# Convolution inputs ahead of the forget gates, rotary products behind them: the order of the input projections

## The reference

```
h = x * (1 + scale1) + shift1
p = h @ w_in[l]                     # 3088 columns: qa 512, ka 128, va 128, qkv_b 768, g_b 256,
                                    # beta/alpha 16, f_fw 256, f_bw 256, i_c 256, q_c 256, g_c 256
qkv_b = silu(short_conv(qkv_b, conv_w))              # width 5, centred, per channel
f = lb + (1 - lb) * sigmoid(z);  log_f = log(f)      # z = (f_fw, f_bw); in layer 0 lb = 0
o_a = attn_latent(rope_2d(qa), rope_2d(ka), va, cache_k, cache_v, sink)
x = LayerNorm(alpha*x + gate1 * (concat(attention, gated DeltaNet, HGRN2) @ w_out[l]))
x = LayerNorm(alpha*x + gate2 * FFN(...))            # layer 0 SwiGLU, layer 1 top-2 of 8 experts
```

## Time and profile before

| | us |
|---|---|
| median of 3 runs | 2377.2 (2377.14 to 2379.05) |
| the profiled execution, its span | 2378.1 |
| input projection of layer 0, from 67 to 235 us | 168 |
| attention of layer 0, with the rest of `w_mod`, from 235 to 365 us | 130 |
| input projection of layer 1, from 1156 to 1317 us | 161 |
| TensorE busy over the span | 2118.8 (89%) |
| VectorE, ScalarE, GpSimd busy over the span | 1449.5, 1283.3, 754.2 |

### The profile page before, as it was taken

The page is one execution under the profiler, slowest core; times in us unless marked ns, Lnnn a source line. Parts: engine busy times, 40 slices in busy tenths (PEclk is TensorE's granted clock), DMA queues, the critical chain, the costliest instruction groups (busy, mean ns, idle before and its releaser), DMA issues.

```text
span 2378.1 us, 54636 instructions
## 1 busy us (share of the span) xinstructions
PE 2118.8 (89%) x23130; PEld 1305.1 (55%) x23130; DVE 1449.5 (61%) x1797; ACT 1283.3 (54%) x1665; POOL 754.2 (32%) x556
## 2 busy tenths in 40 slices
PE   5999787978989999999899878878869999999994
PEld 3756456745565555555675558645544444444442
DVE  3254656668261221215558667595379999999985
ACT  3443554556453333423543665465368877778763
POOL 0332115433404242423233236422023333333332
PEclk8999898988999999999999989998979999999997
DMA  9352680020303131315231000100456777990014
GB/s 285 121 174 77 212 285 28 4 58 8 106 17 106 53 106 53 106 53 166 77 103 39 1 10 4 41 21 22 140 223 223 238 265 276 330 335 34 36 65 183
DMA packets 215529, 278.48 MB, mean 117 GB/s; under 512 B 28321, under 2 KB 188941, under 8 KB 215183
## 3 DMA queue, kind: packets, MB, share of 16 engines
q1 hardware_dynamic: 203776, 243.60, 31.5%
q0 software_dynamic: 8432, 29.89, 3.4%
q10 hardware_dynamic: 3103, 1.85, 0.3%
HBM read 368.36 MB, written 29.11 MB: 167 GB/s over the span
## 4 chain that ended last, share of the span: by engine, by line
PE 53%; issue 16%; DVE 13%; POOL 8%; ACT 7%; DMA 2%; SPq 1%; POOLq 0%; DVEq 0%; ACTq 0%
PE ps L2328 50%; POOL mix L1000 6%; DVE mix L1695 1%; DVE arena L1687 1%; DVE mix L1687 1%; DMA wbuf<-in_w_mod 1%; POOL mix L1003 1%; DVE small L1910 1%; DVE arena L1691 1%; SPq L727 1%; DVE mix L1849 1%; DMA const<-in_w_mod 1%; ACT mix L1461 1%; PE ps L3097 1%; PE ps L3073 1%
## 5 line engine op out<-in xcount | busy, mean ns | idle before, releaser
L2328 PE MATMUL ps<-hT,mix 128*128 128x512 f16 (+2 forms) x3024 | 376.7, 287 | 25.0 <-DVE hT L1687 11.8
L2328 PE MATMUL ps<-w,xgT 128*128 128x512 f16 x1632 | 366.3, 381 | 5.3 <-DVE w L2228 5.3
L2228 DVE SCALAR_TENSOR_TENSOR w<-wst,w 128x2048 f16<-128x2048 f32 x136 | 309.8, 2318 | 25.6 <-ACT w L1558 25.5
L2328 PEld LDWEIGHTS ps<-hT,mix 128*128 128x128 f16 x3024 | 227.1, 99 | 172.9 <-issue 22.2
L1032 POOL TENSOR_TENSOR a<-aval,a 128x256 f16<-128x256 f32 x68 | 158.3, 2328 | 370.4 <-ACT a L1606 370.4
L2328 PEld LDWEIGHTS ps<-w,xgT 128*128 128x128 f16 x1632 | 157.7, 98 | 184.5 <-issue 9.6
L1558 ACT ACTIVATE w<-wst 128x2048 f16<-128x2048 f32 x136 | 251.5, 1898 | 9.6 <-DMA xs_rows<-htok,slot_i 9.6
L2328 PE MATMUL ps<-mix 128*128 128x512 f16 (+5 forms) x1856 | 204.7, 288 | 15.7 <-POOL mix L1003 8.8
L2328 PE MATMUL ps<-hT,arena 128*128 128x128 f16 (+1 forms) x1440 | 200.7, 300 | 1.1 <-DVE const L1687 1.1
L2328 PE MATMUL ps<-w2m,aT 128*128 128x512 f16 x816 | 187.2, 379 | 3.8 <-DVE aT L2266 3.8
L2328 PEld LDWEIGHTS ps<-mix 128*128 128x128 f16 (+3 forms) x1856 | 121.3, 123 | 90.4 <-POOL mix L1003 12.4
(11 more groups left out here) (359 smaller groups left out, 3546.3 us busy)
## 6 DMA issues: line engine op xcount, KB each, us to landing
wst<-in_moe_w SPq DMA_DIRECT2D x204, 1024.0 KB
wbuf<-in_w_mod SPq DMA_DIRECT2D x40, 1024.0 KB
wbuf<-in_ffn_w SPq DMA_DIRECT2D x33, 1024.0 KB
wbuf<-in_w_in SPq DMA_DIRECT2D x20, 1024.0 KB
xs_rows<-in_table SPq DMA_DIRECT2D x17, 512.0 KB, 6.4
ys_rows<-yb POOLq DMA_DIRECT2D x17, 512.0 KB, 4.2
wbuf<-in_w_out SPq DMA_DIRECT2D x32, 256.0 KB
xg<-xs_rows POOLq DMA_DIRECT2D x16, 512.0 KB, 5.5
```

What stands on the lines that cost most here:

```text
L2228: v_.scalar_tensor_tensor(out=q[1], in0=staged(s, p), scalar=WS, in1=q[0], op0=ALU.mult, op1=ALU.subtract).then_inc(sg["m_lo13"], 1)
L2328: return mm_(o, w, x, start=first, stop=last, skip_group_check=True)
```

## The change

```diff
-MOD_AT = {j: i for i, j in enumerate(("va", "f0b", "f1b", "b1", "b3", "b5", "gb1", "ckt"))}
-TURN_AT = {"b3": 0, "gc0": 1}
-MOD_FETCH = {"f0": 0, "f1": 1, "b0": 2, "b1": 3, "b2": 4, "ba": 5, "i": 6, "gc": 7}
+MOD_AT = {j: i for i, j in enumerate(("va", "b1", "b3", "b5", "f0b", "f1b", "gb1", "ckt"))}
+TURN_AT = {"f0b": 0, "gc0": 1}
+MOD_FETCH = {"b0": 0, "b1": 1, "b2": 2, "f0": 3, "f1": 4, "ba": 5, "i": 6, "gc": 7}
...
-        j = [f"q{t}" for t in range(4)] + ["ka", "va", "f0a", "f0b", "f1a", "f1b"] + [f"b{t}" for t in range(6)]
-        j += ["gb0", "gb1", "ba", "ia", "ib", "kout", "ckt"] + [f"rot{t}" for t in range(5)]
+        j = [f"q{t}" for t in range(4)] + ["ka", "va"] + [f"b{t}" for t in range(6)]
+        j += ["f0a", "f0b", "rot0", "rot1", "f1a", "f1b", "rot2", "rot3", "rot4"]
+        j += ["gb0", "gb1", "ba", "ia", "ib", "kout", "ckt"]
         j += ["gc0", "gc1", "qc0"]
...
-        j = ["qa0", "qa1", "kv", "f0", "f1", "b0", "b1", "b2", "gb", "ba", "i", "gc", "qc"]
+        j = ["qa0", "qa1", "kv", "b0", "b1", "b2", "f0", "f1", "gb", "ba", "i", "gc", "qc"]
...
 # ScalarE
+                for t in range(6):        # pad <- b0..b5, upper: b2, f0, f1
+                for h in range(2):        # exp f0, upper gb; exp f1, upper ba
+                upper(l, "i")
...
 # VectorE
+                for t in range(6):
+                    if l == 0 and t % 2:
+                        row_of(f"b{t}")
+                    L.done(J(f"b{t}"))    # then the five taps
...
+                def rotated(t):
+                    s = L.full(J(f"rot{t}"))
+                    tt(rtmp, s[:, 0:LAT], sinT, ALU.mult, job=J(f"rot{t}"))
+                    tt(qk[:, t, 0:LAT], qk[:, t, 0:LAT], cosT, ALU.mult)
+                    tt(qk[:, t, 0:LAT], qk[:, t, 0:LAT], rtmp, ALU.add, to="rope_ready")
...
+                for t in range(2):
+                    rotated(t)
+                if l == 0:
+                    row_of("f1b")
+                for t in range(2, 5):
+                    rotated(t)
                 L.done(J("f1b"))          # then the forget-gate block
...
+                if l == 0:
+                    row_of("gb1")
+                ts(ba[:, :, :], L.full(J("ba"))[:, 0:80].rearrange("p (t n) -> p t n", t=TT), IWS, ALU.mult, job=J("ba"))
...
 # TensorE
+                def rotate(t):
+                    s = open_(J(f"rot{t}"))
+                    close(mm(s[:, 0:LAT], rot, qk[:, t, 0:LAT]), J(f"rot{t}"))
+
+                for t in range(6):
+                    project(l, f"b{t // 2}", J(f"b{t}"), (t % 2) * P, h2)
+                    mods_at(f"b{t}")
+                L.done(J("ka"))
+                for p_, turned_ in (("f0", range(2)), ("f1", range(2, 5))):
                     w = split_piece(l, p_)
                     tokens(J(p_ + "a"), w, (0, 256), range(4))
                     tokens(J(p_ + "b"), w, (0, 256), range(4, 5))
                     mods_at(p_ + "b")
+                    for t in turned_:
+                        rotate(t)
```

More of the change, by code:

```diff
@@ L593, in wpiece @@
             return wbuf[:, slot, 0:8 * n].rearrange("p (k n) -> p k n", k=KT)
-        IN_PIECES = ["qa0", "qa1", "kv", "f0", "f1", "b0", "b1", "b2", "gb", "i", "gc", "qc"]
+        IN_PIECES = ["qa0", "qa1", "kv", "b0", "b1", "b2", "f0", "f1", "gb", "i", "gc", "qc"]
         OUT_PIECES = ["wo0", "wo1", "wo2", "wo3"]
@@ L1119, in _ @@
                     copy(qk[:, t, :], L.full(J(f"q{t}"))[:, 0:NT], J(f"q{t}"), IWS)
-                upper(l, "f0")
+                upper(l, "b0")
                 copy(qk[:, 4, :], L.full(J("ka"))[:, 0:NT], J("ka"), IWS)
                 copy(va[:, :, :], L.full(J("va"))[:, 0:NT].rearrange("p (t n) -> p t n", t=TT), J("va"), IWS)
-                upper(l, "f1")
+                upper(l, "b1")
                 if l == 0:
@@ L1129, in _ @@
                     L.do(a.activation(alog[:, :], alog[:, :], ACT.Exp), "lb_exp")
[L1130 to L1135, removed]
                 L.need("pad_zero")
@@ L1142, in _ @@
                     if t % 2:
-                        upper(l, ("b2", "gb", "i")[t // 2])
-                    if t == 3:
-                        upper(l, "ba")
+                        upper(l, ("b2", "f0", "f1")[t // 2])
+                for h in range(2):
+                    for part, t0, t1 in (("a", 0, 4), ("b", 4, 5)):
+                        j = J(f"f{h}{part}")
+                        s = L.full(j)[:, 0:(t1 - t0) * 256].rearrange("p (t n) -> p t n", n=256)
+                        L.free(a.activation(lf[:, t0:t1, h * 256:(h + 1) * 256], s, ACT.Exp, scale=-IWS), j)
+                    upper(l, ("gb", "ba")[h])
+                upper(l, "i")
                 for t in range(2):
@@ L1838, in _ @@
                     tt(lbt[:, :], lbt[:, :], lbrow[:, 1], ALU.mult)
+                for t in range(6):
+                    if l == 0 and t % 2:
+                        row_of(f"b{t}")
+                    L.done(J(f"b{t}"))
+                    for w in range(CONV):
+                        at = P + 64 + (l * CONV + w) * 6 + t
+                        if w == 0:
+                            ts(cv[:, t, :], pad[:, t, 0:CVW], par[:, at:at + 1], ALU.mult)
+                        else:
+                            stt(cv[:, t, :], pad[:, t, w:w + CVW], par[:, at:at + 1], cv[:, t, :], ALU.mult, ALU.add,
+                                to="conv_done" if (t, w) == (5, CONV - 1) else None)
+                def rotated(t):
[3 more added lines that the diff above has]
+                    tt(qk[:, t, 0:LAT], qk[:, t, 0:LAT], rtmp, ALU.add, to="rope_ready")
                 if l == 0:
+                    chunk_of(TURN_AT["f0b"])
                     row_of("f0b")
+                dve.wait_ge(sg["rope_in"], 16 * (l + 1))
+                for t in range(2):
[4 more added lines that the diff above has]
+                    rotated(t)
                 L.done(J("f1b"))
                 if l == 0:
-                    row_of("f1b")
                     ts(lfd, lfd, 1.0, ALU.add, 1e30, ALU.min)
@@ L1892, in _ @@
                     row_of("ckt")
[L1893 to L1898, removed]
                 if l == 0:
@@ L2450, in _ @@
                 mods_at("va")
-                for p_ in ("f0", "f1"):
+                def rotate(t):
[6 more added lines that the diff above has]
+                for p_, turned_ in (("f0", range(2)), ("f1", range(2, 5))):
                     w = split_piece(l, p_)
@@ L2455, in _ @@
                     mods_at(p_ + "b")
-                for t in range(6):
-                    project(l, f"b{t // 2}", J(f"b{t}"), (t % 2) * P, h2)
-                    mods_at(f"b{t}")
+                    for t in turned_:
+                        rotate(t)
                 for t in range(2):
@@ L2472, in _ @@
                 mods_at("ckt")
-                for t in range(5):
-                    s = open_(J(f"rot{t}"))
-                    close(mm(s[:, 0:LAT], rot, qk[:, t, 0:LAT]), J(f"rot{t}"))
                 for t in range(2):
```

## The result

| | us |
|---|---|
| changed kernel, median of 16 runs | 2384.75 (2380.98 to 2391.79) |
| kernel before, median of 16 runs beside it | 2379.72 (2377.14 to 2385.83) |
| ratio | 1.0021, 95% interval 1.0011 to 1.0031 |
| forecast | 2383.1, range 2374.5 to 2387.0 |

The changed kernel is 5.0 us slower by the ratio, between 2.6 and 7.4. The profiled execution of the changed kernel has a span of 2380.8 us.

The account below looks back on a forecast made before the run. The prediction took TensorE's matmul queue to bound both input projections, with VectorE's copy of ba decisive in layer 1. Layer 0 -2.4 and layer 1 +8.3 gave +5.9 us: 2383.1 us from 2377.2, range 2374.5 to 2387.

Parts of the forecast that it names:

- Layer 0, forecast -2.4: Layer 0 input projection: TensorE's gap of 2.45 us behind kout goes, gain 2.4 us, bounds 0 to 2.45.
- Rival C: Layer 0's gain is lost in the attention to late w_mod pieces, layer 1 stalls as forecast: 2385.5 us, chance 0.12.
- Layer 1, forecast +8.3: Layer 1 input projection: TensorE waits at ckt for VectorE's copy of ba, 7.5 us plus 0.8 for the clock, bounds 0 and 9.2.
- The signs that the prediction named: Layer 1: one 13 to 15 us gap, gc0 7 to 9 us later, two stretched VectorE instructions, clock 0.50; layer 0: gc0 earlier.
- The rotations 2 to 4 with their collision: Layer 1, VectorE behind f1b: 6.5 us clean, with a GpSimd collision ending at 1267.6 instead of 1264.2.
- the gate block: Layer 1, VectorE between rotations and copy of ba: 31.0 us clean, with a collision from 1267.6 to 1302.6.
- the two collisions: Layer 1: GpSimd's lower of i holds up VectorE's rotations, its lower of qc the short instructions behind the three products.
- my placing: Layer 1, TensorE jobs placed from ScalarE's rows: f0b ends 1241.8, rot0 and rot1 1243.7, f1b 1256.8, rot2 1257.7, rot4 1259.6.
- The clock term: Layer 1 behind the gap at ckt: TensorE's low clock costs 0.8 us more than before, bounds 0 and 1.7.
- Rival A: The GpSimd collisions miss VectorE in layer 1: layer 1 about 0, layer 0 -2.4, 2374.8 us; with one, 2379; chance 0.23.
- Rival B: Layer 1: TensorE does not wait at ckt; 10.6 us gained with layer 0's 2.4, 2366.6 us, chance 0.08.

Follow-up runs that it names:

- e1: Changed kernel, but in layer 1 VectorE copies ba right behind the reciprocal of the gate block: 2373.4 us, ratio to the kernel before 0.9964.
- e8: Changed kernel, but in layer 1 ba is copied ahead of the last three short instructions of the gate block: 2379.54 us in one run.
- e7: The kernel of e1 run a second time, unchanged, for its trace: 2368.67 us in its one run.
- e4: Changed kernel, but in layer 1 GpSimd starts lower i only after the rotations and lower qc only after the gate block: 2377.39 us, ratio 0.9989.
- e5: Kernel before with only the rotary products moved between and behind the f jobs, and layer 1's ba copied one b job earlier: 2372.25 us, ratio 0.9975.

## Why the prediction was right

*What bounds it.* TensorE, with VectorE behind the copy of ba. Shown by e1, in time and trace, and by the gap of e8: one instruction of 0.24 us, placed earlier, moves the kernel by 0.57% (1.0021 to 0.9964).

*Layer 0, forecast -2.4.* The projection is 2.62 us shorter, 0.2 more than the upper bound of 2.45; where those 0.2 come from is open. Rival C, a loss to late pieces of `w_mod`, falls: TensorE waits no longer for them than before. From 220 to 640 us, before and changed (engine and what it waited for: us in total, times, longest):

```profile
PE ps L2328 <- DMA wbuf<-in_w_mod: 4.0, 3, 2.0
PE ps L2333 <- DMA wbuf<-in_w_mod: 3.6, 2, 2.0
```

The attention of layer 0, measured like that of layer 1 in e1, takes 140.8 us instead of 139.7, within the 2 us that the prediction allowed. Such a difference says little: e1 and e7, the same kernel, have 144.4 and 140.8.

*Layer 1, forecast +8.3: right in mechanism, 1.8 us too large* (measured 177.79 - 171.27 = 6.52). The signs that the prediction named came, but for one: gc0 starts 6.5 us later, counted from the start of the stage, and not the 7 to 9 us that it asked for. The steps: the gap was to be 13 to 15 us and is 13.72. The rotations 2 to 4 with their collision were put at 9.9 us (1257.7 to 1267.6) and took 9.6 (1253.31 to 1262.88); the gate block at 35.0 and took 34.6. Each of the two collisions came where it was placed. The `lower` of ba, put at 0.9 us within these rotations, took 0.43 us and stretched none of them. The f jobs and the rotary products between them came 0.3 us sooner than my placing. These steps make 1.0 us. The other 0.8 us, for a longer stay at the low clock, were not spent: 21.26 against 21.20 us.

*The sum.* Forecast +5.9; the two projections of the profiled executions give +3.9, the ratio +5.0 (2.6 to 7.4). The clock term and the placing are the mis-sized ones. The median of 2384.75 and the forecast of 2383.1 do not compare directly, since the kernel before read 2379.72 beside it, 2.5 us above the 2377.2 that the forecast started from; +5.0 on 2377.2 is 2382.2.

*Rival A* (the collisions miss) did not happen, but its size was right: without them the changed kernel is at 0.9989, where A had 2374.8 of 2377.2, 0.9990. *Rival B* (no wait at ckt) did not happen either, the wait was there; but it was worth what was worked out: forecast 2366.6 of 2377.2, 0.9955; e1, which takes the wait away, has 0.9964 (0.9952 to 0.9976), and part of the difference is its low clock in the i job.

The collisions are shown by e4: with GpSimd held back, both stretches go. The rule of the Trainium skill, "GPSIMD Engine Reference", Specifications, that GpSimd's SBUF interfaces are shared with VectorE and contend with its instructions in a two-port mode or with two SBUF inputs, agrees with the stretched rotations (two SBUF inputs: 3.76 and 4.49 us for 0.69). The stretched instruction of 5.23 us and the copy of 3.92 us in e4 have one SBUF input; by the rule they run in a two-port mode, which the traces do not show. The rotation instruction that reads PSUM started inside a `lower` of 4.07 us once in the changed kernel, at 1257.67, 0.13 us into it, and took its 0.69 us; the same row of e1, e7 and e8 took 0.69 us too.

*What beats both kernels.* The changed order with ba copied behind the reciprocal (e1): 0.9964 of the kernel before. e5 (0.9975) reaches the same lengths of the projections, but for the clock that e1 lost in the i job (155.18 and 162.46 us, against 155.19 and 163.92 in e7), and their intervals overlap; which of the two is the faster stays open.

## What to carry to other kernels

When jobs take buffers in turn, a short copy that frees one belongs as early in its engine's program as its data allows. Before moving a block of work, list which small frees stand behind it and who takes those buffers next; here a 0.24 us copy that stood behind the gate block, 34.6 us long, and not within it, turned a gain of some 9 us (0.9964 of 2380) into a loss of 5. A reordering that is right for the busiest engine should be tried with each part alone and with the frees moved: two parts at 0.998 and 1.000 gave 1.002 together and 0.996 with the free in its place.

## What the runs showed that I had not expected

The granted clock of TensorE can fall while its row shows it busy without a pause. Behind the ba job (120 matmuls of 16 columns in 3.17 us) it was at 0.50 for some 3 us in five cases of twenty, and each time the next job took 1.6 to 1.7 us longer. Neither the cause nor what decides between the cases was tried.

GpSimd waits too. In e4 its `lower`, started 0.1 us after a VectorE instruction of 1.49 us had begun, took 5.32 us instead of 4.07. And the reciprocal, 16.15 us on one SBUF input, neither held up a `lower` that started inside it nor was held up, in layer 1 of all ten kernels.
